# The feed-forward gate's row of a hybrid layer: its sums over partitions from two rounded parts, at another place of the output projection

## What is computed

```
mod = silu(c) @ w_ada + b_ada                 # c: [1, 1024], w_ada: [1024, 6144]
shift_m, scale_m, gate_m, shift_f, scale_f, gate_f = split(mod, 6)
...
y = merged @ w_out                            # merged: [256, 1024]
x = x + gate_m * rmsnorm(y, g_mix_post)
h2 = rmsnorm(x, g_ff_pre) * (1 + scale_f) + shift_f
y2 = square(relu(h2 @ w_ff1)) @ w_ff2
return x + gate_f * rmsnorm(y2, g_ff_post)
```

## Time and profile before

| | us |
|---|---|
| median of three runs | 818.89 |
| lowest and highest | 817.93, 819.17 |
| the profiled execution, its own time | 818.6 |
| its span, first to last instruction | 817.2 |

### The profile page before, as it was taken

One profiled execution on the slowest core, in us unless ns is written; L12 is line 12 of the kernel. 1 busy time (PEld: TensorE's weight loads), 2 busy tenths in 40 slices (PEclk: granted clock), 3 DMA queues, 4 the chain that ended last, 5 costly groups with the idle time before them and its releaser, 6 DMA issues.

```text
span 817.2 us, 12179 instructions
## 1 busy us (share of the span) xinstructions
PE 790.9 (97%) x4838; PEld 696.3 (85%) x4838; DVE 570.5 (70%) x772; ACT 427.8 (52%) x636; POOL 92.0 (11%) x145
## 2 busy tenths in 40 slices
PE   3999999999999999999999999999999999999997
PEld 2899988999879888888889998888987988888885
DVE  4886988969978475665567899858545766556564
ACT  5445266753455574444456467647445644444452
POOL 6300980001110000000001000011001100000001
PEclk9999999999999999999999999999999999999999
DMA  9978977777545656655656554445533566566551
GB/s 306 363 248 271 372 256 251 251 259 263 189 156 182 205 183 192 192 173 190 195 188 194 176 171 147 144 155 189 173 106 127 170 198 198 182 189 196 183 180 51
DMA packets 83608, 163.64 MB, mean 200 GB/s; under 512 B 5457, under 2 KB 13841, under 8 KB 83553
## 3 DMA queue, kind: packets, MB, share of 16 engines
q1 hardware_dynamic: 81632, 157.31, 59.2%
q10 hardware_dynamic: 1424, 4.81, 1.7%
q0 software_dynamic: 496, 0.76, 0.3%
HBM read 161.81 MB, written 1.05 MB: 199 GB/s over the span
## 4 chain that ended last, share of the span: by engine, by line
PE 85%; DVE 7%; ACT 4%; issue 2%; DMA 1%; POOL 1%; SPq 0%; ACTq 0%; DVEq 0%; POOLq 0%
PE bank L1783 20%; PE bank L1785 19%; PE bank L1784 19%; PE bank L1814 13%; PE bank L1816 6%; DVE ada_acc L984 2%; DVE lo_ring L952 2%; PE bank L1989 1%; ACT hi_ring L501 1%; PE bank L2338 1%; PE bank L2359 1%; PE bank L1852 1%; DMA ada_ring<-in_w_ada 1%; PE bank L2008 1%; DVE x_residual L1067 1%
## 5 line engine op out<-in xcount | busy, mean ns | idle before, releaser
L952 DVE TENSOR_TENSOR lo_ring<-raw_ring,hi_ring 128x1024 fp32r<-128x1024 f32 x248 | 306.3, 1240 | 160.4 <-ACT hi_ring L501 159.9
L501 ACT CAST hi_ring<-raw_ring 128x1024 fp32r<-128x1024 f32 x248 | 258.6, 1049 | 264.2 <-PE bank L1785 170.6
L1783 PE MATMUL bank<-h_hi_lo,hi_ring 128*128 128x256 f32 x560 | 163.9, 293 | 3.3 <-DVE lo_ring L952 1.9
L1814 PE MATMUL bank<-h_hi_lo,hi_ring 128*128 128x512 f32 x448 | 158.7, 398 | 0.0
L1784 PE MATMUL bank<-h_hi_lo,hi_ring 128*128 128x256 f32 x560 | 158.3, 283 | 0.0
L1785 PE MATMUL bank<-h_hi_lo,lo_ring 128*128 128x256 f32 x560 | 158.3, 283 | 0.0
L1783 PE MATMUL bank<-hi_ring,branch_hi 128*128 128x512 f32 x320 | 126.6, 396 | 0.0
L1816 PE MATMUL bank<-h_hi_lo,lo_ring 128*128 128x256 f32 x448 | 125.8, 281 | 0.0
L1785 PE MATMUL bank<-hi_ring,branch_lo 128*128 128x512 f32 x320 | 124.8, 390 | 0.0
L1784 PE MATMUL bank<-lo_ring,branch_hi 128*128 128x512 f32 x320 | 124.6, 389 | 0.0
L1783 PEld LDWEIGHTS bank<-h_hi_lo,hi_ring 128*128 128x128 f32 x560 | 107.1, 191 | 7.8 <-DVE lo_ring L952 3.1
(11 more groups left out here) (272 smaller groups left out, 1031.9 us busy)
## 6 DMA issues: line engine op xcount, KB each, us to landing
raw_ring<-in_w_ff SPq DMA_DIRECT2D x128, 512.0 KB, 4.0
raw_ring<-in_w_in SPq DMA_DIRECT2D x64, 512.0 KB, 4.5
raw_ring<-in_w_out SPq DMA_DIRECT2D x16, 512.0 KB, 3.4
raw_ring<-in_w_xkv SPq DMA_DIRECT2D x16, 512.0 KB, 3.6
mem_v<-in_w_ada SPq DMA_DIRECT2D x12, 512.0 KB, 6.8
ada_ring<-in_w_ada SPq DMA_DIRECT2D x10, 512.0 KB, 6.0
mem_k<-in_w_ada SPq DMA_DIRECT2D x10, 512.0 KB, 5.4
raw_ring<-in_w_branch SPq DMA_DIRECT2D x8, 512.0 KB, 4.6
```

The lines of the kernel that those rows point to most:

```text
L501: act.copy(m.hi[:, m.slot(u)], m.raw[:, m.slot(u)]).then_inc(s.hi_done, 1)
L952: dve.tensor_tensor(m.lo[:, m.slot(u)], m.raw[:, m.slot(u)], as_f32(m.hi[:, m.slot(u)]), ALU.subtract).then_inc(s.lo_done, 1)
L1783: pe.matmul(out, a_hi, b_hi, start=start, stop=False, skip_group_check=True)
L1814: pe.matmul(b, m.hi[:, slot, k, fc], x_both[:, k0 + k].rearrange("p a s -> p (a s)"), start=first and k == 0, stop=False, skip_group_check ...
```

## The change

- TensorE's two fp32 matmuls of the row behind unit two go. In their place four fp32r matmuls stand behind unit four: ones times the high part and ones times the low part, for each half, accumulated in the same banks 4 and 5. They wait for `row_lo`.
- ScalarE rounds slabs 2 and 3 of `ada_acc` (128x1024) into `br_hi[:, 4:8]`, ahead of the rounding of unit five; VectorE subtracts to get the low part into `br_lo[:, 4:8]`, where `ada_row` was. These buffers held the inputs of the branch products, which are over then (`s.used >= OUT`).
- VectorE's `ada_row` (bias and gain) comes behind the loop, after the low part of unit eight and before the scaling of the second half's first tile.
- The matrix of ones is declared as fp32r and read as fp32 elsewhere. Two semaphores are new.

```diff
+        self.row_hi, self.row_lo = new("ff_row_hi"), new("ff_row_lo")
...
-        self.ones = sb("ones", [P])
+        self.ones_r = sb("ones", [P], F32R)
+        self.ones = as_f32(self.ones_r[:, :])
...
+        self.row_sum_hi, self.row_sum_lo = self.br_hi[:, 4:8], self.br_lo[:, 4:8]
...
     act.dma_start(m.mem, t["mem_2"][0].rearrange("(a p) d -> p a d", p=P)).then_inc(s.mem_in, DMA)
+    act.wait_ge(s.ada_used, ADA_UNITS)
+    act.wait_ge(s.used, OUT)
+    act.copy(m.row_sum_hi.rearrange("p a s -> p (a s)"),
+             m.ada_acc[:, 2:4, :].rearrange("p a n -> p (a n)")).then_inc(s.row_hi, 1)
     for j in range(RING):
...
         if j == 2:
-            ada_row(s.ff_row_ps, s.ff_rows_in, s.ff_row, m.rows[:, 1, :], 4)
+            dve.wait_ge(s.row_hi, 1)
+            dve.tensor_tensor(m.row_sum_lo.rearrange("p a s -> p (a s)"),
+                              m.ada_acc[:, 2:4, :].rearrange("p a n -> p (a n)"),
+                              as_f32(m.row_sum_hi).rearrange("p a s -> p (a s)"), ALU.subtract).then_inc(s.row_lo, 1)
         after(OUT + j)
+    ada_row(s.ff_row_ps, s.ff_rows_in, s.ff_row, m.rows[:, 1, :], 4)
...
         tokens(OUT + j, UK * j, m.h_hi, m.h_lo, OUT_BANKS[0][0], j == 0, j == RING - 1, beside=ff_cols if j == 0 else None)
-        if j == 1:
-            pe.wait_ge(s.ada_used, ADA_UNITS)
-            ada_row(2, 4).then_inc(s.ff_row_ps, 1)
+        if j == RING - 1:
+            claim(4, 5)
+            pe.wait_ge(s.row_lo, 1)
+            for i in range(2):
+                for part in (m.row_sum_hi, m.row_sum_lo):
+                    mm = pe.matmul(bank[4 + i][:, :], m.ones_r[:, :], pair(part, 2 * i), start=part is m.row_sum_hi,
+                                   stop=part is m.row_sum_lo)
+            mm.then_inc(s.ff_row_ps, 1)
             free[4], free[5] = (s.ff_row, 1), (s.ff_row, 3)
```

## The result

The changed kernel takes 820.32 us in the median of eight runs (819.84 to 821.64), against 819.03 us of the kernel before (817.93 to 819.25, eight runs). The ratio is 1.0023, 95% interval 1.0014 to 1.0032. That is about 1.9 us slower by the ratio; the two medians lie 1.3 us apart. The forecast was 819.8 us, a ratio of 1.0011: the direction and the time lie within what was said, but by the ratio the loss is twice as large as the sum gave.

A forecast was written before the change was run, and what follows sets the result against it. TensorE bounds the kernel (85% of the chain; VectorE 7%). Four added matmuls 0.91 less 0.04 give 0.87 us, ScalarE and VectorE 0; on the median 818.89 that is 819.76, say 819.8 us, range 818.0 to 820.9.

The forecast's parts named there:

- TensorE, removed: Output projection, ahead of unit three: taking out the row's 1.88 us of fp32 matmuls gains 0 to 0.1 us, taken as 0.
- TensorE's clock falls in the uncovered wait: Rival, 8%: TensorE idles some 1.85 us ahead of unit three, units three and four run at the slow pace; 822.0 us.
- The price of the fall: Loss if units three and four run at the slow clock: 2.2 us, taken from slow matmuls at the kernel's start.
- The row lay in a wait: Ahead of unit three TensorE waits for VectorE's L1271 anyway, so removing the row's matmuls gives 0.1 us at most.
- in the way after all: Rival, 8%: the row's fp32 matmuls delayed unit three by their full 1.88 us; 0.97 us faster, 817.9 us.
- The four matmuls: Four fp32r matmuls added on TensorE behind unit four, where nothing hides them: 0.91 us, bounds 0 and 1.88 us.
- The swallowed gap: At unit eight, TensorE's short wait for its low part disappears as TensorE arrives later: worth 0.04 us.
- ScalarE and VectorE at nothing: ScalarE's added rounding copy (about 1.0 us) and VectorE's added subtraction (1.22 us) and moved operations are hidden: cost 0.
- The rival of a late low part: Rival, 4%: the row's low part reaches TensorE late, behind unit four; 0.2 us in the end, 820.0 us.
- The 0.15 us: VectorE's four moved operations, after unit eight's low part, end 0.15 us past the old wait; hidden by TensorE's 0.87 us delay.
- The delay is absorbed: Rival, 10%: a later step, such as ScalarE's queue or a feed-forward load, has room; no change, 818.9 us.
- last per cent: Chance said to remain, beyond the forecast and its rivals, for the 1.2 us spread of three runs.

The follow-up runs named there:

- run with VectorE's low part late: Kernel before, with VectorE's weight-unit low part moved behind the merged activations' low parts in the branch products' second half; 818.24 us, ratio 0.9999.
- run without the row: Changed kernel with seven matmuls without use ahead of unit three and the row's four matmuls behind unit four left out; 818.77 us, ratio 1.0005.

## Why the prediction was wrong, point by point

**What failed is the step "TensorE, removed".** The sum took it as 0. That is right for the time at which unit three is released and wrong for the pace at which it then runs: the idle time that is left made the granted clock fall to 0.50, and units three and four took 1.57 us more in the profile (1.59 us in the second). The prediction had this mechanism with its place, "TensorE's clock falls in the uncovered wait", and held it unlikely (8%): "here the engine was busy on both sides". It had two rows to go by, the 3.08 us at the start, before slow matmuls, and the 1.04 us ahead of the feed-forward, before fast ones, and its chance is that of the second. The runs put the difference between them: 1.41 us is like the second, 1.85 us like the first in nine of fifteen executions. Being busy on both sides did not prevent it.

**The price of the fall** was put at 2.2 us from the start of the kernel. The three profiles with a fall have 1.57, 1.59 and 1.57 us; the groups give 1.7 us (820.47 against 818.78) and 2.0 (821.64 against 819.67, one execution). The forecast with a fall, 822.0, was built on 818.89, the late kind; most falls came in early executions, which are 1 us shorter. So it is luck that the measured median, 820.32, lies inside the range and only 0.5 us above the forecast: a fall and an early start partly cancel.

**The row lay in a wait:** right. Removing it released unit three no earlier: 2.25 us behind the last start of unit two, against 2.24. The run with VectorE's low part late shows that VectorE held the third unit for 0.4 us beyond the row, where the prediction had 0.1 us at most. The rival "in the way after all" is out.

**The four matmuls:** right, 0.91 us in the trace, from 227.62 to 228.53, and 0.6 to 1.2 us by the groups. **The swallowed gap:** 0.04 us forecast, 0.08 between unit five and the feed-forward.

**ScalarE and VectorE at nothing:** right. The roundings of units five and six end at 222.16, where 222.8 less the 0.52 of the start was worked out; VectorE waits 0.24 us for the first; the row's low part is ready 2.6 us before TensorE wants it (223.80 and 1.22 us, against 227.62), more than the 1.0 us forecast because the slow clock holds TensorE up; and behind the moved operations 0.67 us remain, where 0.7 was worked out (the slow clock moved these and the squares alike). The rival of a late low part is out. The 0.15 us by which the operations would not fit without the delay is what the run without the row shows.

**"The delay is absorbed":** out; from the feed-forward's start to the end both profiles take 571.4 to 571.5 us, and doubling the row doubles the loss.

**The chances:** the forecast's 70% and the rivals' 8, 10, 8 and 4% make 100, so there are no "last per cent" left for the spread of the runs.

The Trainium skill, page "TensorE: Matmul & The Clock Gate", section "Part 1: The HAM clock gate (the "warmup" mystery)", has the two levels that the rows show here (0.43 and 0.228 us for 512 columns, granted 0.50 and 1.00). The prediction used it for the rival and not for its chance.

## What to carry to other kernels

Work that lies in another engine's wait costs nothing, and on TensorE it may even be worth something, as here: before taking it out, look for what else keeps the engine going, and price the idle time that is left by the longest one in the trace that did no harm. Where the trace has no such idle time, the question is open and deserves a chance that fits, not the one of the nearer row. Matmuls moved from such a wait to a place where TensorE sets the pace count in full, however much cheaper they have become.

## What the runs showed of the hardware

- An idle time of TensorE of 1.85 us between dense stretches brought a granted clock of 0.50 in nine of fifteen executions, one of 2.06 us in eight of eleven. One of 1.41 us did so in none of eleven, one of 0.94 us in none of eleven.
- The fall came with the first matmul behind the idle time in one profile, 0.6 us later in a second and 1.0 us later in a third, and was over at about 224.0, 224.3 and 225.0 us. It cost 1.57, 1.59 and 1.57 us, by the distance from unit three to unit five.
- Two fp32 matmuls of 128x512 are recorded as four, with 1.88 us, but counted back from the next matmul's start they took 1.71 us (in the run with VectorE's low part late).
- The first 20 us of the kernel have two courses that differ by 1 us in the end, in every kernel here. In the twelve profiles the eight column sums at 14.4 to 14.8 us took 1.83 or 1.84 us in the seven late ones and 1.02 us in the five early ones. Why an execution takes the one or the other stays open, and so does why falls in the changed kernel came mostly with the early course (eight of nine, with no early one spared) while in the kernel before without the row they came with both, and three early ones were spared.
